# The last normalisation moved from after the expert loop into it

## The reference

```
h   = layer_norm(alpha*h + mixer(h))                 # h1, 2048 x 1024
probs = softmax(h @ w_router)                         # 16 experts, 4 groups of 4
group = argmax over groups of (sum of its best two)   # one group for each token
two experts of that group, gates normalised to sum 1
y(token) = gate1 * expert1(h) + gate2 * expert2(h)    # expert: (silu(x w1) * (x w3)) w2
out = layer_norm(alpha*h + y, ln2_g, ln2_b)
```

## Time and profile before

| | |
|---|---|
| runs | 1493.08 us median of 3 (1492.92 to 1497.52) |
| the profiled execution | 1497.2 us, of which the span of the profile is 1495.7 us |
| busy: TensorE, DVE, ACT, POOL | 1327.1, 828.2, 525.7, 299.8 us |
| mean rate of all DMA | 162 GB/s |
| expert loop | about 700 to 1414 us |
| final phase | from the last matmul, about 1414 us, to 1495.7 us |

### The profile page before, as it was taken

How to read it: one execution, slowest core, us unless ns; L and a number is a source line. 1 busy time by engine, 2 the same in 40 slices (tenths; PEclk the granted TensorE clock), 3 DMA queues, 4 the chain that set the end, 5 groups by cost and what they waited for, 6 DMA issues and landing times. The chain is left out here.

```text
span 1495.7 us, 19094 instructions
## 1 busy us (share of the span) xinstructions
PE 1327.1 (89%) x6300; PEld 1110.0 (74%) x6301; DVE 828.2 (55%) x997; ACT 525.7 (35%) x583; POOL 299.8 (20%) x301
## 2 busy tenths in 40 slices
PE   2999999999999999805999999999999999999700
PEld 2888888888888888705888888888888888888600
DVE  6567585758575843694444552433533524535277
ACT  3323233323432341220344442433533424434222
POOL 3001010102010100450121121111211111111178
PEclk9999999999999999756999999999999999999955
DMA  7625445544453444250475775563665546763283
GB/s 196 179 86 167 141 127 183 183 127 140 168 182 99 142 162 174 106 203 26 154 224 153 225 219 154 164 212 89 224 200 165 168 146 171 222 211 95 56 315 140
DMA packets 145552, 243.02 MB, mean 162 GB/s; under 512 B 8464, under 2 KB 74016, under 8 KB 145520
## 3 DMA queue, kind: packets, MB, share of 16 engines
q1 hardware_dynamic: 123520, 171.98, 35.2%
q0 software_dynamic: 17968, 55.94, 14.3%
q10 hardware_dynamic: 4032, 14.68, 2.6%
HBM read 199.05 MB, written 52.43 MB: 168 GB/s over the span
## 5 line engine op out<-in xcount | busy, mean ns | idle before, releaser
L460 PE MATMUL acc<-ring_hi 128*128 128x512 f32 x768 | 302.3, 394 | 1.5 <-DVE ring_lo L949 1.5
L462 PE MATMUL acc<-ring_hi,ring_lo 128*128 128x512 f32 x768 | 299.9, 390 | 0.0
L461 PE MATMUL acc<-ring_lo,ring_hi 128*128 128x512 f32 x768 | 299.6, 390 | 0.0
L460 PE MATMUL acc<-ring_hi,xt_hi 128*128 128x512 f32 x640 | 253.7, 396 | 2.4 <-DVE xt_lo L1244 2.4
L462 PE MATMUL acc<-ring_hi,xt_lo 128*128 128x512 f32 x640 | 250.3, 391 | 0.0
L461 PE MATMUL acc<-ring_lo,xt_hi 128*128 128x512 f32 x640 | 250.1, 391 | 0.0
L1265 DVE TENSOR_TENSOR ring_lo<-stage_x,ring_hi 128x2048 fp32r<-128x2048 f32 x60 | 134.8, 2289 | 103.9 <-ACT ring_hi L707 103.6
L460 PEld LDWEIGHTS acc<-ring_hi 128*128 128x128 f32 x768 | 144.8, 188 | 31.1 <-issue 1.9
L462 PEld LDWEIGHTS acc<-ring_hi,ring_lo 128*128 128x128 f32 x768 | 144.6, 188 | 30.5
L461 PEld LDWEIGHTS acc<-ring_lo,ring_hi 128*128 128x128 f32 x768 | 144.9, 189 | 29.2
L1326 POOL TENSOR_TENSOR rstd<-vareps,half 128x1 f32<-128x1 f32 x32 | 47.8, 1494 | 463.8 <-DVE vareps L919 463.8
(11 more groups left out here) (213 smaller groups left out, 1619.6 us busy)
## 6 DMA issues: line engine op xcount, KB each, us to landing
stage_x<-in_exp_w SPq DMA_DIRECT2D x64, 1024.0 KB, 7.4
stage<-in_w_in SPq DMA_DIRECT2D x64, 512.0 KB, 5.4
stage<-in_exp_w SPq DMA_DIRECT2D x32, 1024.0 KB, 7.0
stage<-in_w_out SPq DMA_DIRECT2D x32, 512.0 KB, 5.0
h_scratch<-hres POOLq DMA_DIRECT2D x16, 512.0 KB, 3.0
sum_scratch<-hres ACTq DMA_DIRECT2D x16, 512.0 KB, 3.8
f_rows<-sum_scratch SPq DMA_DIRECT2D x16, 512.0 KB, 9.3
out<-f_rows SPq DMA_DIRECT2D x16, 512.0 KB, 2.6
```

The costliest lines, as they stand in the source:

```text
L460: nc.tensor.matmul(dst, w_hi, x_hi, start=start, stop=False)
L461: nc.tensor.matmul(dst, w_hi, x_lo, start=False, stop=False)
L462: return nc.tensor.matmul(dst, w_lo, x_hi, start=False, stop=stop)
```

## The change

Everything of the final phase is done within the loop. Each block reads back the sums of its tokens as they stand, adds its own result, and always computes the normalised rows as well. Rows whose token has another block still to come go back to `sum_dram`; rows whose token is complete go to `out`. Two lists of indices, `put_first` and `put_last`, carry out-of-bounds numbers for the rows that are not theirs. For that, a token's number in `dest` carries a mark for its later expert. Experts are taken in another order, the first of each group, then the second of each and so on, so that three experts of other groups lie between two neighbours of one group. SP's loop over experts becomes straight code and its final loads and stores go.

```
-            def put(b):                     # pool: adds yrow onto sum_dram by an indirect DMA
-            def put_done(puts):
+            def gather_sums(b):
+                G.tensor_copy(sum_now[:], token[:, bass.ds(b, 1)]).then_inc(s_sn, 1)
+                pool.wait_ge(s_sn, b + 1)
+                pool.wait_ge(s_y, b + 1)
+                if not (isinstance(b, int) and b < 2):
+                    pool.wait_ge(s_put, b * 16 - 16)
+                G.indirect_dma_start(srow[:], None, sum_dram, ... sum_now ...).then_inc(s_sgat, 16)
+            def put_sums(b):
+                if not (isinstance(b, int) and b == 0):
+                    pool.wait_ge(s_put, b * 16)
+                G.tensor_copy(put_now[:], put_first[:, bass.ds(b, 1)]).then_inc(s_pn, 1)
+                pool.wait_ge(s_pn, b + 1)
+                pool.wait_ge(s_y, b + 2)
+                G.indirect_dma_start(sum_dram, ... put_now ..., rrow[:], None).then_inc(s_put, 16)
+            def final_root(b):
+                pool.wait_ge(s_fve, b + 1)
+                G.tensor_tensor(frstd[:], fve[:], half[:], ALU.pow).then_inc(s_fr, 1)
+            def final_put(b):
+                if not (isinstance(b, int) and b == 0):
+                    pool.wait_ge(s_store, b * 16)
+                G.tensor_copy(out_now[:], put_last[:, bass.ds(b, 1)]).then_inc(s_on, 1)
+                pool.wait_ge(s_fn, b + 1)
+                G.tensor_tensor(nrow[:], nrow[:], b_2[:], ALU.add).then_inc(s_fo, 1)
+                pool.wait_ge(s_on, b + 1)
+                pool.wait_ge(s_fo, b + 1)
+                G.indirect_dma_start(out_rows, ... out_now ..., nrow[:], None).then_inc(s_store, 16)
+            def next_rows(b):
+                pool.wait_ge(s_xt, b * 2 + 4)
+                pool.wait_ge(s_gat, b * 16 + 32)
+                gather(b + 2)
+            def block_end(b, more):
+                put_sums(b)
+                final_root(b)
+                if more:
+                    gather_sums(b + 1)
+                final_put(b)
             with pool.Fori(2, nb1) as b:
-                gather(b + 2); put_done(b - 1); put(b - 1)
+                next_rows(b)
+                block_end(b - 1, True)
```

```
+            def final_rows(b):              # dve, in turn(b + 1): after w1, hid_rows, x_lo, w3, before w2
+                dve.wait_ge(s_sgat, b * 16 + 16)
+                if not at0: dve.wait_ge(s_put, b * 16)
+                dve.wait_ge(s_w2, b + 2)
+                for n in range(2):
+                    cols = slice(n * 512, (n + 1) * 512)
+                    ins = V.tensor_tensor(rrow[:, cols], srow[:, cols], acc[2 + n][:], ALU.add)
+                ins.then_inc(s_y, 1)
+                dve.wait_ge(s_y, b + 2)
+                V.bn_stats(fstats[:, 0, :], rrow[:, 0:512])
+                V.bn_stats(fstats[:, 1, :], rrow[:, 512:1024]).then_inc(s_fst, 1)
+                V.bn_aggr(fmv[:], ...).then_inc(s_fst, 1)
+                if not at0: dve.wait_ge(s_fr, b)
+                V.tensor_scalar(fve[:], fmv[:, 1:2], EPS, None, ALU.add).then_inc(s_fve, 1)
+                if at0: dve.wait_ge(s_fg, 32)
+                else:   dve.wait_ge(s_store, b * 16)
+                V.scalar_tensor_tensor(out=nrow[:], in0=rrow[:], scalar=fmv[:, 0:1], in1=g_2[:],
+                                       op0=ALU.subtract, op1=ALU.mult).then_inc(s_fm, 1)
```

```
-            def y_rows(b):                  # act: two copies of 128 x 512
+            def final_scale(b):             # act, in turn(b + 2), between hid_hi and silu
+                act.wait_ge(s_fr, b + 1)
+                act.wait_ge(s_fm, b + 1)
+                nc.scalar.mul(nrow[:], nrow[:], frstd[:]).then_inc(s_fn, 1)
+            act.wait_ge(s_plist, 1)         # before turn 0
+            act.dma_start(g_2[:], bc(ln2_g[0])).then_inc(s_fg, 16)
+            act.dma_start(b_2[:], bc(ln2_b[0])).then_inc(s_fg, 16)
```

```
-    w1_v = exp_w1[0].rearrange("e (k p) f -> e p k f", p=P)          # w3, w2 alike
+    w1_v = exp_w1[0].rearrange("(g i) (k p) f -> i g p k f", p=P, g=NEG)
-            with sp.Fori(1, NE) as ex:
+            for ex in range(1, NE):
...
+            tt(gs_d[:, 0:NT], row_d[:], row_a[:], ALU.is_gt)          # routing, 128 x 16 each
+            V.scalar_tensor_tensor(out=dest[:, 0, :], ... scalar=LAST ...)
+            ch.mark(V.scalar_tensor_tensor(out=dest[:, 1, :], ... scalar=-LAST ...))
```

More of the change, by code:

```diff
@@ L362, in build @@
         s_y = sem("y_rows")
+        s_szero = sem("srow_zeroed")
+        s_sn = sem("sum_index")
+        s_sgat = sem("sums_gathered")
         s_pn = sem("put_index")
-        s_put = sem("y_put")
-        s_yfree = sem("y_rows_free")
-        s_allput = sem("all_rows_put")
+        s_put = sem("sums_put")
+        s_on = sem("out_index")
+        s_plist = sem("put_lists")
         s_fg = sem("ln2_in")
-        s_fh = [sem(f"final_in{t}") for t in range(NT)]
+        s_fst = sem("final_stats")
         s_fve = sem("final_var_eps")
         s_fr = sem("final_rstd")
+        s_fm = sem("final_scaled")
         s_fn = sem("final_normed")
-        s_fm = sem("final_scaled")
         s_fo = sem("final_rows")
@@ L439, in _ @@
                     load_expert(ex, j)
[L442 to L453, removed]
         @block.tensor
@@ L882, in _ @@
             x_hi(0)
+            act.wait_ge(s_plist, 1)
+            act.dma_start(g_2[:], bc(ln2_g[0])).then_inc(s_fg, 16)
+            act.dma_start(b_2[:], bc(ln2_b[0])).then_inc(s_fg, 16)
             turn(0, True)
-            with act.Fori(1, nb) as b:
+            turn(1, False)
+            with act.Fori(2, nb) as b:
                 turn(b, False)
             hid_hi(nb - 1)
[L887 to L894, removed]
+            final_scale(act.value_load(nblocks[0:1, 2:3], min_val=NE - 2, max_val=NB - 2))
+            final_scale(act.value_load(nblocks[0:1, 1:2], min_val=NE - 1, max_val=NB - 1))
         @block.vector
@@ L1280, in turn @@
                 if not first:
+                    final_rows(b - 1)
                     with dve.If(ended > 0):
@@ L1286, in _ @@
             turn(0, True)
-            with dve.Fori(1, nb) as b:
+            turn(1, False)
+            with dve.Fori(2, nb) as b:
                 turn(b, False)
             hid_lo(nb - 1)
[L1292 to L1306, removed]
+            final_rows(dve.value_load(nblocks[0:1, 1:2], min_val=NE - 1, max_val=NB - 1))
         @block.gpsimd
@@ L1427, in gather @@
                                      bounds_check=SEQ - 1, oob_is_err=False).then_inc(s_gat, 16)
-            def put(b):
+            def gather_sums(b):
+                G.tensor_copy(sum_now[:], token[:, bass.ds(b, 1)]).then_inc(s_sn, 1)
+                pool.wait_ge(s_sn, b + 1)
+                pool.wait_ge(s_y, b + 1)
+                if not (isinstance(b, int) and b < 2):
+                    pool.wait_ge(s_put, b * 16 - 16)
+                carry(pool, s_pool_past)
+                G.indirect_dma_start(srow[:], None, sum_dram, bass.IndirectOffsetOnAxis(ap=sum_now[:, 0:1], axis=0),
+                                     bounds_check=SEQ - 1, oob_is_err=False).then_inc(s_sgat, 16)
@@ L1447, in _ @@
             gather(0)
+            G.memset(srow[:], 0.0).then_inc(s_szero, 1)
+            pool.wait_ge(s_szero, 1)
+            gather_sums(0)
             pool.wait_ge(s_gat, 16)
@@ L1450, in _ @@
             gather(1)
+            pool.wait_ge(s_plist, 1)
+            next_rows(0)
             nb1 = pool.value_load(nblocks[0:1, 1:2], min_val=NE - 1, max_val=NB - 1)
             nb2 = pool.value_load(nblocks[0:1, 2:3], min_val=NE - 2, max_val=NB - 2)
[L1453 to L1459, removed]
-            with pool.Fori(2, nb1) as b:
[L1461 to L1469, removed]
+            next_rows(1)
+            block_end(0, True)
+            with pool.Fori(2, nb1) as b:
+                next_rows(b)
+                block_end(b - 1, True)
+            block_end(nb2, True)
+            block_end(nb1, False)
             pool.wait_ge(s_gat, nb * 16 + 16)
             pool.wait_ge(s_put, nb * 16)
[L1472 to L1477, removed]
-                G.tensor_tensor(frstd[:, i:i + 1], fve[:, i:i + 1], half[:], ALU.pow).then_inc(s_fr, 1)
-            def final_bias(t):
-                i = t
-                pool.wait_ge(s_fn, t + 1)
-                G.tensor_tensor(f_rows[:, i, :], f_rows[:, i, :], b_2[:], ALU.add).then_inc(s_fo, 1)
-            for t in range(NT + 1):
-                if t < NT:
-                    final_root(t)
-                if t >= 1:
-                    final_bias(t - 1)
+            pool.wait_ge(s_store, nb * 16)
 _INS = ["x", "ln_in_g", "ln_in_b", "w_in", "pool_w", "pool_scale", "conv_w", "conv_b", "w_out", "ln1_g", "ln1_b",
```

108 lines of the change are left out of this document (66 added, 42 removed).

## The result

The changed kernel takes 1456.88 us in the median of four runs (1455.42 to 1460.65), against 1495.3 before: ratio 0.9747, 95% interval 0.9731 to 0.9763. It is faster by 38 us where 60 were forecast, and lies outside the range of 1427 to 1451. The profiled execution took 1455.42 us with a span of 1453.7, 42.0 less than the span before.

What follows compares the result with a forecast made beforehand. It took TensorE to bound the loop and POOL the final phase, 81.5 us in the open. 65.4 - 2.9 - 1 - 0.4 - 1 = 60.1 us saved gave 1433.0 us, own range 1428 to 1441, stated range 1427 to 1451.

Steps and rivals of the forecast that it cites:

- Behind the last matmul: After TensorE's last matmul: one tile's chain instead of 16, 16.1 us left of 81.5, so 65.4 us saved.
- The DMA and the closing behind it: End of the kernel: landing of the last out write 5.0 us (2.6 to 6.1), closing of the program 1.8.
- The last `down`: Last block: it waits for hid_lo, now behind DVE's final_rows of the block before; 2.9 us lost.
- The clock's fall: Last matmuls: TensorE's idle gap may drop the clock to 1.2 GHz; 2 us or 0, taken as 1.
- Routing: Routing stage before the loop: three operations on 16 columns, 0.18 us each, one fewer in the lists; 0.4 us lost.
- Waits in dense blocks: Loop, six periods with w2, w1 and w3 units together: TensorE stalls 0 to 0.5 us each; 1 us taken, bounds 0 and 10.
- rival 4: Six dense blocks: the skill's DVE and POOL exclusion at its dearest, 1.1 us each, 1439 us; shares the forecast's 71%.
- A block takes 17.7 us: Loop: the block's period, read from the kernel before, was expected to stay 17.7 us after the change.
- Its other sign: Whole kernel: the prediction called itself wrong if the span shrinks by less than 45 us.
- Rival 1: Loop: late landings of indirect transfers hold up DVE's fixed order, costing 20 to 30 us, 1453 to 1463; 24%.
- Rival 2: Loop: POOL's turn in each block becomes the bound and the kernel gets slower, 1513 us at 19.7 us a block; 3%.
- Rival 3: Loop: a wait chains one block's normalisation to TensorE's next turn, 1.5 us lost per block, 1490 to 1496 us; 2%.

Runs made afterwards that it cites:

- d1_bias_on_dve: d2_last_hid_lo with the normalisation's last multiplication (ACT) and bias addition (POOL) joined in one DVE operation after hid_lo of the next block: 1434.66 us, ratio 0.9583.
- a2_no_bias_add: a1_arena_back without POOL's bias addition onto nrow, so b_2 is missing from the output: 1438.43 us, ratio 0.9618.
- d2_last_hid_lo: a1_arena_back with the last block's hid_lo placed on DVE between the additions and statistics of the block before: 1444.34 us, ratio 0.9647.
- b1_arena_moved: The kernel before with an unused tile of 64 bytes per partition ahead of the arena, moving it up by 128 bytes: 1514.32 us, ratio 1.011.
- b2_interleaved_only: The kernel before with only the interleaved order of experts, SP's loop unrolled and the routing's operations permuted to match: 1496.75 us, ratio 1.0001.
- e1_arena_256: The kernel before with the arena moved up by 256 bytes: 1493.45 us in one run.
- a1_arena_back: The changed kernel with its two new index tiles placed inside the arena, which starts at its old address, 128 bytes lower: 1446.64 us, ratio 0.9670.

## Why the prediction was wrong

By its own steps, forecast and measured (profiled executions):

- Behind the last matmul: 65.4 forecast, 64.1 measured. The chain up to the out DMA was right. The DMA and the closing behind it, 5.0 and 1.8 by the prediction, took 3.3 and 4.7: POOL's wait for the landing (L1524) ends at 1449.0, 3.3 behind the issue, and then comes a step of the closing on POOL's queue that I had no term for:

```profile
L116 POOLq DRAIN  x1: 4242/4242/4242, 1449.2 to 1449.2; - x1
```

d1_bias_on_dve and a2_no_bias_add have the same two parts, 3.3 and 4.7. Before, this step ended at 1495.4, 4.1 us behind POOL's last addition, and the last store landed within it; that is why the closing looked like 1.8. So the sum is only 1.2 us off here because two terms missed in opposite directions.
- The last `down`: 2.9 forecast, 2.8 (4.7 for 1.9). The clock's fall, 1 of 0 or 2: it came, and cost 2.6 with 13 matmuls at 0.63 us. d2_last_hid_lo and d1_bias_on_dve had a wait of 1.5 and no fall. The change is not the only way to it, though: b1_arena_moved and b2_interleaved_only have the old 1.9 us wait there, and the granted clock was 0.50 during a part of the last matmuls all the same (last block 10.0 and 9.9 us instead of 8.3).
- Routing: 0.4 lost forecast, 4.5 gained. Most likely not the change's doing. The granted clock falls at 619.5 us in the profile before and at 624.7 in the one after, while TensorE makes the logits; in the eleven profiles of this study a fall at 619.5 to 621.1 us goes with a first transpose of the loop at 696.2 to 697.8, one at 622.3 to 624.7 with 692.6 to 693.7, and kernels with the changed loop and with the old one are found on both sides (d1_bias_on_dve and e1_arena_256 among the late ones, a1_arena_back among the early). So of the 42.0 us between the two profiles only 38.4 stand in the medians. The forecast took the profiled execution before to lie 4.1 us above the median; that median was of three runs, and against the four of the result it is 1.9.
- Waits in dense blocks: 1 us forecast, 5.6 measured and 9.4 with the pace restored. The mechanism was named: POOL's reads and DVE's ring units exclude each other, and the limit is 18.1 us after the accumulators are ready. Its size was wrong: 0.6 in each of four of the six dense blocks, 0.9 in one and 2.3 in the one with the late put, where rival 4 had 1.1 at the dearest. I had let only the bias addition meet the units. The rows show POOL's other steps held up too (1.83 for a copy of 0.18, 2.15 for an issue of 1.06), and so the addition came later, beside the w1 units, which lost 2.9 us to it instead of 1.7.
- **The step that failed: "A block takes 17.7 us".** The prediction carried the period over and looked only for waits. It became 18.10 without any wait, 15.9 us in 39 blocks, the largest part of the 22 us that were missing. The diff had the cause in sight, two tiles ahead of `aligned("arena_pad")`, in a kernel that aligns its tiles to 128 bytes, and the prediction has no term for them. None of the rivals was about matmuls that become slower. With the address restored a1_arena_back lies within the range, at 1446.6: 49.0 us saved of 60.1, and of the 11 that are still missing 8.4 are stalls. The prediction had said that TensorE waiting over 0.3 us in blocks that aren't dense would prove it wrong; they didn't wait at all, and it was wrong all the same. Its other sign, a span that shrinks by less than 45 us, came true with 42.0, and the last matmul ended at 1436.4 where 1416 to 1425 was forecast.

Rival 1 (landings in the loop) did not occur: gathers of sums landed in 4.4 us in the median, 9.0 at most, and none of the waits that the trace of the kernel after names for DVE is for them. Its price rested on a misread row: the 15.4 of the earlier trace rows is the last load into `f_rows` in the final phase, and the 40 puts of the loop took 4.5 to 9.7. Rival 2 (POOL as the bound) did not: POOL was busy 122.4 of 200 us in the loop. Rival 3 (1.5 us lost in every block through a chain of waits) did not either: each block did lose 0.41 us, but without a wait. That d1_bias_on_dve came out at 1434.7, 1.7 above the forecast, doesn't bear the sum out: it also lacks the late `hid_lo`, the clock's fall and two steps of the chain that the sum had priced.

## What to carry to other kernels

A tile of a few bytes can cost more than the work that comes with it, if it shifts what TensorE reads: compare the start-to-start time of matmuls before and after every edit that touches the memory plan, since busy time, waits and clock all look innocent. Where DVE and POOL both read rows from SBUF in one tight window, count every POOL instruction there, index copies and indirect DMA issues included, and give the row work to one of them. Work that is brought out of a serial end into a loop should leave the last turn its own order, and then the next input in line (here the gather of sums) becomes the limit.

## What the runs showed of the hardware

- Matmuls of 128 x 512 float32 in this three-product form start every 226 to 227 ns, or in turn every 229 and 237 ns (`up`), by the place of their stationary tiles relative to the ring: the same 128-byte half of a stretch of 256 is the fast one, in all eleven profiles. Only shifts of 0, 128 and 256 bytes were tried. Transposes stayed at some 109 ns.
- An indirect DMA's issue on POOL that began while DVE was in an operation with two inputs in SBUF took 2.16 us in the median (29 cases in the kernel after) against 1.04 for the 129 others. Before the change none began so, and its rows don't show it. The Trainium skill ("SBUF — State Buffer", section "Who interferes with whom") has VectorE's tensor_tensor contend with GpSimd's reads, which the copies and the addition bear out, but infers that it leaves the making of DMA descriptors alone; here the measurement decides, and the issue was held up.
- An indirect write without addition took 1.04 us to issue (outside of such a wait), where the adding one took 1.6. It landed in 3.3 us in the median instead of the puts' 6.2, but with some of its rows skipped, so the two landings aren't a fair comparison.
